# Two of each token's eight gated expert rows summed by TensorE through diagonal matrices

## What is computed

```
def swiglu(x, w1, w3, w2):
    return (jax.nn.silu(x @ w1) * (x @ w3)) @ w2

    def expert_block(acc, blk):
        tok, wt, e = blk
        y = swiglu(x_pad[tok], w1[e], w3[e], w2[e])
        return acc.at[tok].add(y * wt[:, None].astype(y.dtype)), None
...
    out = acc[:T] + swiglu(xt, ws1, ws3, ws2)

        x = deepnorm_residual(x, y, gate, ln_g[i, 1], ln_b[i, 1])   # layer_norm(ALPHA * x + gate * y)
```

## Time and profile before

| | |
|---|---|
| median of 3 runs | 3332.89 us (3331.28 to 3334.97) |
| profiled execution | 3326.32 us |
| its span in the trace | 3324.7 us |
| mean granted TensorE clock | 0.946 |

### The profile page before, as it was taken

One profiled execution on the slowest core, in us unless ns is written; L12 is line 12 of the kernel. 1 busy time (PEld: TensorE's weight loads), 2 busy tenths in 40 slices (PEclk: granted clock), 3 DMA queues, 4 the chain that ended last, 5 costly groups with the idle time before them and its releaser, 6 DMA issues. The chain is left out here.

```text
span 3324.7 us, 34451 instructions
## 1 busy us (share of the span) xinstructions
PE 2969.8 (89%) x11396; PEld 1698.6 (51%) x11397; DVE 1124.9 (34%) x2059; ACT 707.2 (21%) x1353; POOL 459.2 (14%) x473
## 2 busy tenths in 40 slices
PE   6989999998589999999983999998579999999964
PEld 3655656566344444444431567657444444444432
DVE  2443433434541111111155444443542111111108
ACT  0131221303111111211112343332111111111111
POOL 0100000000111111111101112211111111111101
PEclk8999999999799999999996999999789999999987
DMA  6524334231458878778772122112557778887735
GB/s 237 172 67 131 96 99 121 75 112 51 187 209 309 310 307 310 309 310 311 290 276 73 45 70 76 50 51 66 200 192 297 307 312 309 319 311 309 304 149 208
DMA packets 185620, 659.70 MB, mean 198 GB/s; under 512 B 35816, under 2 KB 97352, under 8 KB 129632
## 3 DMA queue, kind: packets, MB, share of 16 engines
q1 hardware_dynamic: 128288, 528.20, 42.1%
q0 software_dynamic: 44832, 104.95, 9.2%
q10 hardware_dynamic: 12448, 25.89, 2.6%
HBM read 640.52 MB, written 73.96 MB: 215 GB/s over the span
## 5 line engine op out<-in xcount | busy, mean ns | idle before, releaser
L1360 PE MATMUL moe_py<-weights_w,moe_hT 128*128 128x512 f32 x1096 | 498.4, 598 | 21.9 <-DVE moe_acc L1338 15.2
L1349 PE MATMUL moe_ph<-weights_w,moe_xT 128*128 128x512 f32 x1040 | 467.6, 603 | 3.3 <-DVE moe_xT L1211 1.8
L1349 PE MATMUL moe_pr<-weights_w,moe_xT 128*128 128x512 f32 x1024 | 454.8, 597 | 4.1 <-DVE moe_xT L1211 1.5
L1211 DVE COPY moe_xT<-moe_tx 128x512 f32<-128x512 f32 x128 | 88.5, 692 | 929.2 <-PE moe_tx L1367 929.2
L742 PE MATMUL attn_proj<-core_hT,attn_w_w 128*128 128x512 f32 x768 | 340.0, 604 | 5.9 <-ACT attn_oT L590 3.4
L1360 PEld LDWEIGHTS moe_py<-weights_w,moe_hT 128*128 128x128 f32 x1096 | 199.1, 192 | 223.4 <-issue 214.6
L1349 PEld LDWEIGHTS moe_ph<-weights_w,moe_xT 128*128 128x128 f32 x1040 | 194.7, 192 | 227.4 <-issue 225.8
L1349 PEld LDWEIGHTS moe_pr<-weights_w,moe_xT 128*128 128x128 f32 x1024 | 189.5, 190 | 220.8 <-issue 220.3
L1088 POOL DMA_INDIRECT y_rows<-moe_ysb,moe_yidx x129 | 130.1, 1009 | 1218.9 <-ACT moe_ysb L1042 1176.0
L742 PEld LDWEIGHTS attn_proj<-core_hT,attn_w_w 128*128 128x128 f32 x768 | 148.5, 194 | 190.7 <-issue 186.8
L1935 PE MATMUL gdn_pj<-core_hT,gdn_w_w 128*128 128x512 f32 x512 | 226.8, 597 | 0.0
(11 more groups left out here) (340 smaller groups left out, 3085.7 us busy)
## 6 DMA issues: line engine op xcount, KB each, us to landing
weights_w<-in_expert_w_dram SPq DMA_DIRECT2D x387, 1024.0 KB, 7.4
attn_w_w<-in_attn_w_in_dram SPq DMA_DIRECT2D x36, 1024.0 KB, 8.2
weights_w<-y_rows SPq DMA_DIRECT2D x32, 1024.0 KB, 4.9
attn_ada_w<-in_ada_w_dram POOLq DMA_DIRECT2D x64, 384.0 KB, 5.3
gdn_w_w<-in_gdn_w_in_dram SPq DMA_DIRECT2D x16, 1024.0 KB, 5.8
normNone_w<-in_ada_w_dram SPq DMA_DIRECT2D x8, 1536.0 KB, 6.7
attn_swp<-attn_raw ACTq DMA_DIRECT2D x192, 64.0 KB, 2.0
gdn_ada_w<-in_ada_w_dram POOLq DMA_DIRECT2D x32, 384.0 KB, 3.7
```

What stands on the lines that cost most here:

```text
L1211: nc.vector.tensor_copy(xT[:, slot, 4:8], tx[1][:]).then_inc(xT_dve, 1)
L1349: last = nc.tensor.matmul(out[:], xt(k), w13[:, ws, :, k], start=k == 0, stop=k == KT - 1)
L1360: last = nc.tensor.matmul(py[n][:], hT2[:, b, k], w2[:, wb, k, n * 512:(n + 1) * 512], start=k == 0, stop=k == 1)
```

## The change

The rows k = 0 and 1 of each token are no longer added by VectorE. ScalarE writes two diagonal matrices per tile, the identity times the gates of k = 0 and of k = 1 (`diag`, two sets by turns). TensorE multiplies them with buffer 0 of `yg` and lets the four products, two for each half of the row, run on into the banks `py`, behind the down product; when the last is done it counts `yg_summed`. VectorE starts a tile with k = 2 (buffer 1), goes on to k = 7, and waits for `yg_summed` instead of `sh_y` before it adds the banks. Buffer 0 is now given back to SP by `yg_summed`; the other three by `yg_used`, which counts six rows a tile instead of eight.

```diff
@@ -937,7 +937,8 @@
-    yg_used = sem("yg_used")
+    yg_used, yg_summed, diag_ready = sem("yg_used"), sem("yg_summed"), sem("diag_ready")
+    diag = st.sb("diag", [P, 2, YG, P])
@@ -1008,8 +1009,11 @@
             for m in range(TT * TOPK // YG):
                 t, k = m * YG // TOPK, m * YG % TOPK
-                if m >= NYG:
-                    sp.wait_ge(yg_used, YG * (m - NYG + 1))
+                if k == 0:
+                    if t:
+                        sp.wait_ge(yg_summed, t)
+                elif t:
+                    sp.wait_ge(yg_used, (TOPK - YG) * (t - 1) + k)
                 sp.dma_start(yg[:, m % NYG], y_rows.rearrange("(t p k) d -> p t k d", p=P, k=TOPK)[:, t, k:k + YG])\
                   .then_inc(yg_in[m % NYG], 16)
@@ -1062,6 +1066,10 @@
             further(act, block)
             for t in range(TT):
+                if t >= 2:
+                    act.wait_ge(yg_summed, t - 1)
+                for k in range(YG):
+                    nc.scalar.activation(diag[:, t % 2, k], c.ident[:], ACT.Copy, scale=gate[:, t, k:k + 1]).then_inc(diag_ready, 1)
                 act.wait_ge(sh_h, t + 1)
@@ -1324,16 +1332,16 @@
-                for k in range(TOPK):
-                    n, m = t * TOPK + k, (t * TOPK + k) // YG
+                for k in range(YG, TOPK):
+                    n, m = t * (TOPK - YG) + k - YG, (t * TOPK + k) // YG
                     dve.wait_ge(yg_in[m % NYG], 16 * (m // NYG + 1))
                     src, by = yg[:, m % NYG, k % YG], gate[:, t, k:k + 1]
-                    if k == 0:
+                    if k == YG:
...
-                dve.wait_ge(sh_y, t + 1)
+                dve.wait_ge(yg_summed, t + 1)
@@ -1465,7 +1473,16 @@
                 if t:
                     pe.wait_ge(sh_acc, 2 * t)
-                down(t % 2, 0, sh_y)
+                for n in range(2):
+                    for k in range(2):
+                        nc.tensor.matmul(py[n][:], hT2[:, t % 2, k], w2[:, 0, k, half(n)], start=k == 0, stop=False)
+
+                pe.wait_ge(yg_in[0], 16 * (t + 1))
+                pe.wait_ge(diag_ready, YG * (t + 1))
+                for n in range(2):
+                    for k in range(YG):
+                        last = nc.tensor.matmul(py[n][:], diag[:, t % 2, k], yg[:, 0, k, half(n)], start=False, stop=k == YG - 1)
+                last.then_inc(yg_summed, 1)
```

## The result

Median 3339.75 us over 18 runs, 3331.68 for the kernel before over as many: ratio 1.0028, 95% interval 1.0021 to 1.0035, so 9.3 us slower (7.0 to 11.7).

What follows compares the result with a forecast made beforehand. The prediction took the end of VectorE's last addition in each expert-stage tail to bound the kernel; +4.8 (layer 0) and +6.0 (layer 1), taken as +11, give 3337.3 from the profiled 3326.3, or 3344 us by the median; range 3336 to 3350.

Steps and rivals of the forecast that it cites:

- Which chain ends last: Expert-stage tails: TensorE's sums set the pace, then a load burst and six VectorE rows end each tail; together +10.8 us.
- the 21 us under before: Both tails: saving of 8 x 2.64 us if nobody holds up VectorE; as a rival 3312 us, chance 0.03.
- TensorE, 3.43 us a tile, 14.69 apart: Each tile: four added matmuls take 3.43 us and lengthen TensorE's chain from 11.26 to 14.69 us.
- S1: End of TensorE's sum for tile 0, when tile 1's loads are issued: 1714.7 in layer 0, 3257.7 in layer 1.
- the rival that it falls: Tail: TensorE's added matmuls run at the 1.2 GHz level, +20.6 us on top, 3365 us; chance 0.04.
- The burst: Tiles 1 to 3: four loads issued together after the sum; 7.34 us from issue to first use of the second.
- the estimate of 6.8: Load burst: the Trainium skill's transfer rule makes two loads usable after 6.8 us, the sum 1.1 lower; not adopted.
- The upper end, 8.64: Burst latency seen at layer 1's beginning, 8.64 us; in both last bursts it would make the sum +13.4.
- 180 GB/s: Layer 1's first load burst: said to move only this in its first microsecond, layer 0's being up to speed sooner.
- The sum: Both tails: each ends 48.34 us after S1, +4.8 in layer 0 and +6.0 in layer 1, together +10.8 us.
- The other three loads are not held back: Rival, tiles 1 to 3: loads for k = 2 to 7 go out as buffers free; -2.6 us, 3330 us, chance 0.08.
- only TensorE would be in the way: Step of the rival with loads not held back: VectorE finds its rows, tail ends at S1 + 41.7 us.

Runs made afterwards that it cites:

- e4_twice: Changed kernel with each diagonal matmul done twice; ratio to the kernel before 1.0083, the two tails together +31.4 us.
- e1_order: Changed kernel with the load that waits for TensorE's sum issued last from tile 1 on; ratio to the kernel before 1.0005, tails +2.7 us.
- e3_buffer: Changed kernel, its load order kept, with a fifth buffer for rows k = 0, 1 of tiles 1 and 3; ratio to before 1.0002, tails +2.7 us.
- e2_no_sum: Changed kernel without the four diagonal matmuls per tile, rows k = 0, 1 left out of the output; ratio to before 0.9954, tails -10.0 us.
- e5_hold: Kernel before, with the first load of tiles 1 to 3 held until TensorE's previous down product is done; ratio to before 1.0008, tails +2.3 us.
- v1_late_tiles: Changed kernel with k = 0, 1 summed on TensorE in tiles 2 and 3 alone, tile 3's held load last; ratio to before 0.9975, tails -10.0 us.
- v1_again: Second run of the version with k = 0, 1 on TensorE in tiles 2 and 3 alone; ratio to the kernel before 0.9977, tails -8.3 us.
- v2_three_last: As v1_late_tiles, with three rows of tile 3 (k = 0 to 2) on TensorE instead of two; ratio to before 0.9988, tails -4.0 us.
- v3_order: As v2_three_last, with tile 3's load of k = 0, 1 issued before that of k = 6, 7; ratio to before 0.9965, tails -9.4 us.

## Why the prediction was right, step by step

- **Which chain ends last.** Right: TensorE's sum, then the burst of loads, then six rows. e4_twice shows the first link (20.7 us for 20.6), e1_order and e3_buffer the second. e2_no_sum and e5_hold show that it takes both to be 10 us slower than before: held loads without the longer chain give -10.0 (with VectorE's rows cut) and +2.3 (uncut), the longer chain without held loads +2.7, the two together +10.6. No run has VectorE's rows cut and neither of the two; the 21 us under before that the prediction puts there are an estimate.
- **TensorE, 3.43 us a tile, 14.69 apart**: measured 3.43 and 14.69. **S1** 14.96 us after the second up product in the sum and in the trace (1715.65 - 1700.69). **ScalarE**: 0.396 us a diagonal (median), 0.37 taken, hidden. **The clock**: the rival that it falls did not come; the three sums on the path take 3.60 us each in both layers, and the granted clock is 1.00 over each of them in layer 0.
- **The burst.** 7.34 us taken from the first issue to the first use of the second load; measured 1722.86 - 1715.58 = 7.28, and 7.3 for the last burst of each layer, so the price from the trace held and not the estimate of 6.8. First uses of the second and third load are 2.55 apart (1725.41 - 1722.86), 2.54 taken. The upper end, 8.64, came again, but only in the first burst of layer 1 (3246.44 - 3237.95 = 8.49), where VectorE then waits 8.11 us for TensorE anyway. The prediction's reason for it does not hold. Its 180 GB/s are of the burst's second microsecond, and layer 0 moved no more in its own:

```profile
1697.80:1698.80 1.00, 1.00 (x3) 0.38 (x2) 0.00 (x0) 0.00 (x0) 0.00 (x0) 1.00 0.82 197
```

What differs is the landing of the burst's first load, 6.1 us against 4.8 in the kernel before and 6.0 against 4.8 in the changed one; why, no run shows. That the bursts on the path would have layer 0's latency was a choice between two rows, and it came out well.
- **The sum**: +4.8 and +6.0 forecast, +4.7 and +5.9 in the tails. The time, 3344, was 4.2 us above the median measured: 1.2 because the kernel before came out at 3331.7 instead of 3332.9, 3.0 because the medians lie 8.1 apart where 11 was taken. The forecast's 10.8 is inside the interval of the runs' 9.3.
- **Small misses of the profile forecast**: tile 0 of layer 1 waits 8.11 us, not 7.5, and that of layer 0 2.50, not 3. The hole before tile 2 of layer 1 is 2.00 us, not 3, because VectorE waited 1.29 us inside tile 1 for the last load; TensorE's pace absorbed it. The rest came: 40 rows on L1342, three waits of SP's queue for TensorE a layer, and 0.5 us in all for VectorE in layer 1.
- **A rival was priced wrongly.** "The other three loads are not held back" was given -2.6 us; built (e1_order, e3_buffer) it is +2.7. The step of it that failed is "only TensorE would be in the way": after the last sum but one (that of tile 2) VectorE's own 14.9 us are longer than TensorE's 12.3. It changed no other number of the forecast, and -2.6 or +2.7, the rival is below the 6.7 us that the prediction calls a difference that can be told.

## What to carry to other kernels

Work moved to an engine with spare time must fit into the spare time of each step, not of the stage: here TensorE had 2.8 us a tile and was given 3.4, while the same two rows gain when they are put only into the last two tiles, behind which it has little left to do. When an operand's release moves to another engine, look at what stands behind its next load in the queue, and at how close together the loads then go out: of two that were issued 0.4 us apart the second took 8.3 us to land here and the first 4.9. And follow a rival's chain to its very end, on every engine, as the forecast's own.

## What was not expected of the hardware

TensorE's clock after short pauses. Before tile 3's down product it stood idle 1.71 us in the changed kernel, layer 0, and the product took 3.67 us at a granted clock of 1.00, that is the 2.4 GHz level. In v1_late_tiles, layer 0, it stood idle 2.34 us and the product took 5.37, with a granted clock of 0.69 over that stretch, so for a part of it at the 1.2 GHz level:

```profile
1741.29 5.37 PE L1479 MATMUL moe_py<-weights_w,moe_hT 128*128 128x512 f32 x8 [2.34 <-DVE moe_acc L1347]
```

and its window there (length, busy PE PEld DVE ACT POOL, granted clock, DMA share, GB/s):

```profile
1741.20:1746.70 5.50, 5.37 (x8) 2.03 (x8) 5.39 (x5) 0.00 (x0) 0.00 (x0) 0.69 0.95 392
```

In v1_again the same pause of 2.34 us left the product at 3.67, and the sum after the next pause of 2.21 us took 5.40 at a granted clock of 0.68 instead of 3.6. The same pair stands in v2_three_last and v3_order: after 2.17 us idle in layer 0 the product took 5.37 in the one and 3.67 in the other. So a pause of 2.2 to 2.3 us sometimes cost TensorE 1.7 us here. It reached the end of the tail where VectorE was waiting for that work: v1_again's layer 0 was 55.13 us where v1_late_tiles's was 53.42. No pause of 1.97 us or less before tile 3's down product or sum did it, in either layer of the kernels above. Why the clock fell in the one case and not in the other no run shows.
